# Loading each 2 MB tile of expert weights as two 1 MB transfers, with the products of its first rows waiting for the first transfer alone

## The reference, cut to what matters

```
def ec_moe(x, w_router, w_gate, w_up, w_down):
    cap = CAPACITY_FACTOR * N // N_EXPERTS            # 32 tokens for each of 16 experts
    aff = softmax(x @ w_router)
    gates, idx = top_k(swapaxes(aff, 1, 2), cap)
    xin = x[bidx, idx]
    h = silu(einsum('becd,edf->becf', xin, w_gate)) * einsum('becd,edf->becf', xin, w_up)
    out = einsum('becf,efd->becd', h, w_down) * gates[..., None]
    return zeros_like(x).at[bidx, idx].add(out)
```

## Time and profile before

| | |
|---|---|
| time, median of 3 runs | 1623.82 us (1623.66 to 1624.95) |
| time of the profiled execution | 1623.93 us |
| its span, first to last instruction | 1622.1 us |
| PE busy | 1329.0 us (82% of the span) |
| DVE, ACT, POOL busy | 311.4, 210.5, 74.1 us |
| granted TensorE clock, mean | 0.934 of full speed |
| transfers | 85410 packets, 501.34 MB |

### The profile page before, as it was taken

One profiled execution on the slowest core, in us unless ns is written; L12 is line 12 of the kernel. 1 busy time (PEld: TensorE's weight loads), 2 busy tenths in 40 slices (PEclk: granted clock), 3 DMA queues, 4 the chain that ended last, 5 costly groups with the idle time before them and its releaser, 6 DMA issues.

```text
span 1622.1 us, 19314 instructions
## 1 busy us (share of the span) xinstructions
PE 1329.0 (82%) x8611; PEld 742.9 (46%) x8611; DVE 311.4 (19%) x732; ACT 210.5 (13%) x433; POOL 74.1 (5%) x92
## 2 busy tenths in 40 slices
PE   8999976667667679999877657667679999999998
PEld 6454533223223235665533223223235864888843
DVE  1154201001001002554311001001003032222211
ACT  1131200000000001440200000000001032211100
POOL 1001000000000001440000000000001000000000
PEclk9999998988879899999998888888889999999999
DMA  9917799999999999435799999999999831344100
GB/s 325 364 53 285 292 426 428 427 427 428 427 427 427 427 419 378 172 118 192 285 429 426 429 427 427 426 427 428 426 425 381 280 130 53 125 146 148 75 0 26
DMA packets 85410, 501.34 MB, mean 309 GB/s; under 512 B 6236, under 2 KB 31184, under 8 KB 60752
## 3 DMA queue, kind: packets, MB, share of 16 engines
q1 hardware_dynamic: 82240, 490.10, 74.5%
q0 software_dynamic: 3088, 10.02, 1.8%
HBM read 499.02 MB, written 1.07 MB: 308 GB/s over the span
## 4 chain that ended last, share of the span: by engine, by line
PE 50%; DMA 45%; DVE 2%; ACT 1%; issue 1%; SPq 0%; DVEq 0%; ACTq 0%
DMA weight_ring<-in_moe_w_down 22%; DMA weight_ring<-in_moe_w_up 12%; DMA weight_ring<-in_moe_w_gate 11%; PE bank L1090 9%; PE bank L687 7%; PE bank L726 5%; PE bank L1125 5%; PE bank L704 5%; PE bank L960 4%; PE bank L692 3%; PE bank L992 2%; PE bank L1005 2%; PE bank L644 1%; PE bank L938 1%; PE bank L886 1%; PE bank L1020 1%
## 5 line engine op out<-in xcount | busy, mean ns | idle before, releaser
L960 PE MATMUL bank<-weight_ring,x_tok 128*32 128x256 f32 x3328 | 230.5, 427 | 118.3 <-DMA weight_ring<-in_moe_w_up 91.5
L960 PEld LDWEIGHTS bank<-weight_ring,x_tok 128*32 128x32 f32 x3328 | 111.8, 120 | 232.1 <-issue 94.0
L992 PE MATMUL bank<-weight_ring,xT 128*32 128x512 f32 x832 | 126.1, 737 | 82.1 <-DMA weight_ring<-in_moe_w_down 75.9
L1090 PE MATMUL bank<-xT,weight_ring 128*128 128x256 f32 (+1 forms) x768 | 153.2, 362 | 1.6 <-DVE xT L1425 0.9
L1090 PEld LDWEIGHTS bank<-xT,weight_ring 128*128 128x128 f32 x768 | 136.0, 190 | 18.6 <-ACT xT L1156 2.1
L1005 PE MATMUL bank<-x_tok,xT 128*128 128x512 f32 x256 | 122.9, 624 | 0.0
L687 PE MATMUL bank<-xT,weight_ring 128*128 128x256 f32 x512 | 113.2, 383 | 1.8 <-DMA weight_ring<-in_mlstm_w_in 1.1
L1741 DVE TENSOR_TENSOR xT<-xT,bank 128x256 f32<-128x256 f32 x32 | 13.5, 422 | 488.9 <-PE bank L960 488.9
L687 PEld LDWEIGHTS bank<-xT,weight_ring 128*128 128x128 f32 x512 | 98.2, 192 | 17.4 <-issue 2.4
L992 PEld LDWEIGHTS bank<-weight_ring,xT 128*32 128x32 f32 x832 | 26.8, 122 | 157.1 <-DMA weight_ring<-in_moe_w_down 72.7
L704 PE MATMUL bank<-weight_ring,xT 128*128 128x512 f32 x192 | 88.9, 604 | 2.3 <-DVE norm_rows L1654 0.8
(11 more groups left out here) (234 smaller groups left out, 995.2 us busy)
## 6 DMA issues: line engine op xcount, KB each, us to landing
weight_ring<-in_moe_w_gate SPq DMA_DIRECT2D x52, 2048.0 KB, 45.9
weight_ring<-in_moe_w_up SPq DMA_DIRECT2D x52, 2048.0 KB, 45.7
weight_ring<-in_moe_w_down SPq DMA_DIRECT2D x52, 2048.0 KB, 45.8
phase_room<-in_moe_w_gate SPq DMA_DIRECT2D x12, 2048.0 KB, 45.4
phase_room<-in_moe_w_down SPq DMA_DIRECT2D x12, 2048.0 KB, 46.4
phase_room<-in_moe_w_up SPq DMA_DIRECT2D x12, 2048.0 KB, 46.3
weight_ring<-in_w_up SPq DMA_DIRECT2D x22, 1024.0 KB, 7.6
weight_ring<-in_gla_w_in SPq DMA_DIRECT2D x6, 2048.0 KB, 22.9
```

Source lines behind the costliest of these rows:

```text
L960: last = mm(bank[q * CAP:(q + 1) * CAP, 0:S], xinT[:, 4 * r + k, j * CAP:(j + 1) * CAP], w[:, k, q * S:(q + 1) * S], start=(r == 0 and k = ...
L992: last = mm(PS[i][k * CAP:(k + 1) * CAP, :], hidT[:, 4 * r + k, :], w[:, k, i * 512:(i + 1) * 512], start=(r == 0), stop=(r == 1), skip_gr ...
L1090: last = mm(PS[bank_pair + c // 2][:, at + tokens.start:at + tokens.stop], w[:, k, c * P:(c + 1) * P], xT[:, k, tokens], start=(k == 0), s ...
```

## The change

Each tile of expert weights is loaded by two transfers of 1 MB: rows `k` = 0 and 1 of every partition (a run of 8 KB) and then rows 2 and 3. The first raises a semaphore of its own, `first_rows_landed[slot]`, the second raises `landed[slot]`. PE waits for the first before the products of the tile's rows 0 and 1 and for the second before those of rows 2 and 3. In a `w_down` tile the second wait stands ahead of `k` = 2 of the first half of the columns. All other weights are loaded as before.

```
+    first_rows_landed = [sem(f"first_rows_landed{i}") for i in range(SLOTS + ROOM_SLOTS)]
...
+    def first_rows_arrived(pe, n):
+
+
+        same = [m for base in T_MOE for m in range(base, base + E * TPE) if SLOT_OF[m] == SLOT_OF[n] and m <= n]
+        pe.wait_ge(first_rows_landed[SLOT_OF[n]], 16 * len(same))
...
                 e, c = divmod(i, TPE)
-                load(T_MOE[layer] + i, ws[c // 2][e, c % 2])
+                n, src = T_MOE[layer] + i, ws[c // 2][e, c % 2]
+                free(n)
+                sp.dma_start(slot(n)[:, 0:2 * D], src[:, 0:2 * D]).then_inc(first_rows_landed[SLOT_OF[n]], 16)
+                sp.dma_start(slot(n)[:, 2 * D:], src[:, 2 * D:]).then_inc(landed[SLOT_OF[n]], 16)
...
                 def tile(c):
 
-                    arrived(pe, base + TPE * e + c)
+
+                    first_rows_arrived(pe, base + TPE * e + c)
                     return slot(base + TPE * e + c).rearrange("p (k n) -> p k n", k=4)
...
                         if j == 0 and c == 0 and k % 2 == 0:
                             pe.wait_ge(xin_dve if k else xin_act, 2 * m + r + 1)
+                        if k == 2:
+                            arrived(pe, base + TPE * e + c + r)
                         for q in range(4):
...
                     for i in range(2):
                         for k in range(4):
+                            if i == 0 and k == 2:
+                                arrived(pe, base + TPE * e + 4 + r)
                             last = mm(PS[i][k * CAP:(k + 1) * CAP, :], hidT[:, 4 * r + k, :],
```

## The result

| | before | after |
|---|---|---|
| median of the runs on one chip, us | 1624.19 | 1636.32 |
| span of the profiled execution, us | 1622.1 | 1634.5 |
| packets of the transfers | 85410 | 113059 |

The change makes the kernel slower: the ratio is 1.0078, with a 95% interval of 1.0062 to 1.0094, and the two medians are 12.1 us apart. The forecast was 6.8 us, and 1630.6 us with a range of 1622.8 to 1639.0. The direction, the place and the mechanism were as forecast; the forecast size was little more than half of what came.

What follows compares the result with a forecast made beforehand. It took the expert-weight transfers, 172 tiles on the path, to bound the expert stages. 1623.93 us + 6.8 for shorter runs - 0 for the early start = 1630.7, less 0.1 for the median: 1630.6 us, range 1622.8 to 1639.

Steps and rivals of the forecast that it cites:

- What bounds the stages: Both expert stages go at the speed of arriving tiles, 4.911 us each; 172 tiles lie on the path.
- The early start in mid-course: In mid-stage PE finishes a tile up to 0.96 us earlier, worth nothing behind a queue 9.4 tiles deep.
- the added waits: 192 more waits on PE in the expert stages, some hundredths of a microsecond a layer at the start, taken as nothing.
- The tail: At each stage's end, the last `w_down` tile gains between nothing and 0.48 us a layer; taken as 0.
- The added issues: 192 more load issues on SP, 327 ns each, hidden by the queue; a held SP starves nothing.
- The semaphore write: One more a tile for each engine in the expert loads, price not shown, taken as one packet more.
- The fixed part of a packet: In expert loads, 4.4 ns a packet from 4 KB runs; nine a tile, 40 ns, make 6.8 us over 172 tiles.
- rival A: Dear packet or semaphore write in the expert loads: 82 ns a tile, 14.1 us slower, 1638 us; chance 0.18.
- the 2 KB rows: Projection loads in 2 KB runs, 84.7 ns each at 387 GB/s, giving a fixed part of 9.1 ns.
- the forecast proper: Expert loads slower by a fixed part of 2 to 7 ns a packet, 1630.6 us in all; chance 0.45.
- The signs that hang on this term: Mid-course windows at 424 GB/s with full DMA share; last `w_down` landing some 3.4 us further behind each layer's first free slot.

Runs made afterwards that it cites:

- e3: The changed kernel with its two transfers a tile, but PE waits for both before the tile's first product: 1636.69 us, ratio 1.0084.
- e5: The kernel before, with SP held back so that no more than five expert tiles are under way: 1624.00 us, ratio 1.0004.
- e7: Against the kernel before, two transfers a tile, even and odd partitions, runs of 16 KB, PE waiting for both: 1624.86 us, ratio 1.0011.
- e4: The changed kernel's two transfers a tile, but in runs of 4 KB, with PE waiting for both: 1660.31 us, ratio 1.0229.
- e9: The kernel before, with 70 of 96 tiles a layer loaded in pairs (32 KB runs), the whole last expert in single tiles: 1618.32 us, ratio 0.9967.
- e8: The kernel before, with 74 of 96 tiles a layer loaded in pairs by 4 MB transfers with 32 KB runs: 1626.81 us, ratio 1.0023.
- e2: The kernel before, one transfer a tile, but its halves go to separate SBUF places, giving 8 KB runs: 1636.15 us, ratio 1.0082.

## Why the prediction was right or wrong, point by point

**What bounds the stages: right.** The whole 12.4 us lie in the two streams of 86 tiles, to within a few hundredths in the other parts.

**The early start in mid-course, worth nothing: right.** Shown by e3 for the early start and the added waits together.

**The tail, 0 to 0.48 us a layer, taken as 0: right**, 1.91 us for 1.92 us, and for the reason given: the groups of rows 2 and 3 had all their instructions left.

**The added issues: right in effect.** SP is held by its queue for 2.1 us at an issue, which was said to starve nothing; e5 shows that a queue of 24.5 us is as good as one of 46 us. That the queue would become shallower was not foreseen.

**The semaphore write, taken as one packet: borne out, loosely.** It is about 9 ns a tile by e7, together with the added issue, with an interval from 2 to 19 ns.

**The fixed part of a packet: the step that failed.** The term "I take the nearest size, 4 KB, and its faster window", 4.4 ns, should have been 9 ns. The sum with 9 fixed parts of 8.75 ns is 172 x 79 ns = 13.5 us, near rival A's 14.1 us and the 12.4 us measured. (The 8.75 ns were read from the change itself; e4 and e9 are the runs that tested them.) Rival A, the price of the 2 KB rows, was the one that came about. That the 1636.3 us lie in the range is owed to A's end of it: the forecast proper was a fixed part of 2 to 7 ns. The signs that hang on this term missed too: 421 GB/s came for 424, and 6.3 and 6.6 us a layer for 3.4. The packets (113059 for 113058) and the tail came as foretold. Streams that last for the whole stage give one engine's time for a packet:

| run | GB/s | kernel | ns a packet | fixed part, from this and the next row |
|---|---|---|---|---|
| 32 KB | 431 | e8 | 1216.5 | 11 |
| 16 KB | 427 | before | 613.9 | 8.7 |
| 8 KB | 421 | after, e2 | 311.3 | 9.1 |
| 4 KB | 409 | e4 | 160.2 | |

(ns a packet: 16 engines x bytes / rate. Fixed part: twice the time of the shorter run less that of the longer; 311.3 x 2 - 613.9 = 8.7. The rates are whole GB/s, which leaves some 3 ns of doubt in the first row, 1.5 in the second and 1 in the third; the few semaphore writes are in them.) No row fits 4.4 ns. The 4 KB runs go at 409 GB/s, not at the 418 GB/s of the earlier trace rows. That window was 3 us long, and a burst of 2 MB lasts for 5. How little such a window can tell is seen in the trace after, where the same loads of `w_down_2`, which the change doesn't touch, read as follows:

```profile
1500.00:1503.00 3.00, 3.00 (x16) 2.64 (x15) 2.72 (x7) 0.00 (x0) 0.00 (x0) 1.00 1.02 410
1460.00:1462.00 2.00, 2.00 (x11) 1.77 (x10) 1.31 (x3) 0.00 (x0) 0.00 (x0) 1.00 1.05 428
```

410 and 428 GB/s for one kind of transfer: windows that scatter by 4% were used to read the 2% between the 427 GB/s of one size and the 418 GB/s of the other. The trace before shows the same: two more windows of 3 us in these loads, with the engines busy to 1.00 or more, read 421 and 396 GB/s.

```profile
1459.50:1462.50 3.00, 3.00 (x16) 2.64 (x15) 2.96 (x8) 0.00 (x0) 0.00 (x0) 1.00 1.02 421
1473.00:1476.00 3.00, 3.00 (x15) 2.65 (x14) 2.96 (x9) 0.08 (x1) 0.00 (x0) 1.00 1.00 396
```

The 2 KB rows, which gave 9.1 ns, came in their first row from a steady 5 us of the middle of a stream that was full for 25: five windows of 5 us from 25 to 50 us read 385 to 388 GB/s. The second, 387 GB/s again 1200 us later, is 3 us long, and the 5 us windows around it read 380, 387 and 378. Nearness in size was the wrong ground for choosing a row; the length and steadiness of its window would have been the better one. That the slower of the two windows "may hold the edge of a burst" was argued only; both of them, 414 and 418 GB/s, lay above the 409 GB/s of the long stream.

## What to carry to other kernels

In a stage that is bound by a stream of transfers, count the packets, not the transfers: each one has a fixed price for its engine (here 9 ns on 614 ns), a second transfer a tile costs little (here 2 to 19 ns), and starting the products early gives nothing while the queue is deep. So the lever is the longer run, and the places to leave it out are the ends of the stage, where the size of what lands last decides what PE still has to do behind it, and a long wait for it can bring a lower clock on top (here 3.45 us for a tile that takes 1.93). To price a small rate difference from a trace, take only windows in the middle of streams that are full for tens of microseconds.

## What the runs showed of the hardware that was not expected

A transfer into partitions 0 to 63, followed by one into 64 to 127, moves at 216 GB/s with the DMA share at 1.01; the same with even and odd partitions moves at 427 GB/s. The Trainium skill, "DMA: Bandwidth & Descriptors", section "The descriptor swizzle", states that partitions 0 to 63 lie behind the even ports of SBUF and 64 to 127 behind the odd ones. By that rule, each half transfer reaches half of the ports and halves the rate, and the two traces agree; that it is the ports was not tried by itself.

How much SP has under way depends on the shape of the transfers. In the change 27.0 us of landing time are 27.0 / 4.981 = 5.4 tiles, in e2 with 8 KB runs in one transfer 33 us or 6.6 tiles, in e4 with 4 KB runs 18.5 us or 3.6 tiles (2.0972 MB / 409 GB/s = 5.13 us each), in e7 with 16 KB runs in two transfers 41 us or 8.4 tiles. No single count of packets or of transfers fits all four, and what sets the limit stays open. The DMA share is 1.01 to 1.03 in mid-course in all of them, so the engines did not run dry.
